# An encoder step with a mixture of experts on one core: low parts on one engine, gate and up weights in 4 KB pieces, token transposes strided, one reordering

## The chip, the cores and the metric

The kernel runs on one core of one Trainium2 chip. The metric is device time in microseconds (us). The kernel before took 510.84 us (median of three runs, 509.73 to 511.15). Engines are called PE (TensorE, matrix products; PEld is its loading of the stationary operand), DVE (VectorE), ACT (ScalarE), POOL (GpSimd) and SP (SyncE, which here only issues transfers).

## What is computed

One layer of a hybrid encoder on 544 tokens (512 of a prompt, 32 of a running stream), width 1024: norm, one input projection split between a gated position-mixing group and a stick-breaking attention group, output projection, residual, then a mixture of experts. All arrays are float32. The change touches only the last part:

```python
def hier_moe(x, w_router_group, b_router_group, w_router_expert, b_router_expert,
             w_gate, w_up, w_down):                      # x (544, 1024) after a norm
    ...                                                  # top group of 4, top 2 of its 4 experts
    combine = ...                                        # (544, 16): gate of each chosen expert
    hg = jnp.einsum('nd,edf->nef', xf, w_gate)           # w_gate, w_up (16, 1024, 256)
    hu = jnp.einsum('nd,edf->nef', xf, w_up)
    a = jax.nn.silu(hg) * hu * combine[:, :, None]
    y = jnp.einsum('nef,efd->nd', a, w_down)             # w_down (16, 256, 1024)
```

## The kernel before

Up to about 295 us the kernel does projection, mixing, attention, output projection and router. Then it runs the 16 experts (E = 16) one after another, each on up to 96 (CAP) gathered token rows. A second round for experts with more than 96 tokens exists in the code and is not run with this input.

**Split products.** A float32 product is made of three passes of a faster format (`three_passes`, L1474 to L1477): high part of x by high part of w, high by low, low by high. The high part of a weight is an ACT copy that rounds (`whi`, L943), the low part is raw minus high (`wlo`, L1350 on DVE).

**Units.** Weights are cut into 48 units of 128 x 2048 values (1 MB), three for each expert: two with half of the 1024 input rows each, gate and up columns side by side, and one with w_down. Expert i uses units 3i - 1 and 3i for gate and up (expert 0: units 0 and 1) and unit 3i + 4 for down (the last: unit 47). SP loads them in the order of their numbers into 12 raw buffers (`moe_loads`, L402): each unit is two DMAs of 512 KB, and from unit 12 on it is issued only when the unit two before it has landed (`few_in_flight`, L446) and its raw buffer is free. High and low parts have three buffers each, so the high part of unit u waits until PE has used unit u - 3 (`hi`, L937).

**Tokens.** POOL gathers the rows of expert i + 2 from DRAM (`gather`, L621), PE transposes them in 8 pieces of 96 x 128 (`turn_tokens`, L1750), ACT and DVE make their high and low parts (`tokens_hi`, L945; `tokens_lo`, L1353).

**Order.** Each engine has its own list of work, in program order; semaphores join them. One step i of PE: gate and up, first half of expert i (12 matmuls of 512 columns); transposes of the activations of expert i - 1; second half (12); transposes of the tokens of expert i + 1; down of expert i - 1 (12). DVE in step i: low part of unit 3i + 1, but only its first 1024 columns; `act_lo`; low part of unit 3i + 2; `tokens_lo` of expert i + 1; `times_up`; low part of unit 3i + 3; `out_rows` (half of the down result from PSUM). ACT has the same order with the high parts. POOL in step i: gather of expert i + 2, low part of the second 1024 columns of unit 3i + 1 (`lo`, L639; semaphore `m_lo_pool`, for which PE's `down` waits), store of the rows of expert i - 2.

Step 0 differs: ACT and DVE make the parts of unit 3 ahead of the parts of expert 1's tokens.

After the last expert POOL gathers the two result rows of each token, and DVE adds them to the residual.

Of the kernel before, what the change touches and what calls it, by code (L numbers as in the profile page):

```python
# [25 lines left out]
F32 = mybir.dt.float32  # L26
# [3 lines left out]
P = 128  # L30
# [4 lines left out]
def trunk_step(nc, x_prompt, x_sample, cache_k, cache_v, norm1_g, w_in, gm_v_norm_g, gm_w_s, gm_b_s,  # L35
# [13 lines left out]
    UK = 4  # L49
# [22 lines left out]
    with ExitStack() as ctx:  # L72
# [157 lines left out]
        m_hi, m_lo, m_lo_pool, m_used = sem("m_hi"), sem("m_lo"), sem("m_lo_pool"), sem("m_used")  # L230
# [105 lines left out]
        def _(sp_):  # L336
# [65 lines left out]
            def moe_loads(r):  # L402
# [26 lines left out]
                def first(m):  # L429

                    i = (m + 1) // 3
                    if not isinstance(r, int):
                        if m % 3 == 1:
                            sp_.wait_ge(m_lo_pool, (E + 1) * r - 4 + m // 3)
                            sp_.sem_inc(sp_tick, 1)
                        elif m == NRAW - 1:
                            sp_.wait_ge(m_lo_pool, (E + 1) * r)
                            sp_.sem_inc(sp_tick, 1)
# [14 lines left out]
                def step(i, b):  # L453
# [5 lines left out]
                    sp_.wait_ge(m_lo_pool, (E + 1) * r + i - 3)  # L459
                    sp_.sem_inc(sp_tick, 1)  # L460
# [12 lines left out]
                sp_.wait_ge(m_lo_pool, (E + 1) * r + E - 4)  # L473
                sp_.sem_inc(sp_tick, 1)
# [17 lines left out]
        def _(pool):  # L492
# [109 lines left out]
            def lo_unit(m, c):  # L602

                return pool.tensor_tensor(wlo[SPLIT_OF[m]][:, c], eraw[m][:, c], whi[SPLIT_OF[m]][:, c].bitcast(F32), ALU.subtract)

# [4 lines left out]
            def moe_gathers(r):  # L610
                s0, u0 = E * r, 3 * E * r
                first = isinstance(r, int)

                if not first:
                    for m in range(3):
                        pool.wait_ge(m_hi, u0 + m + 1)
                        pool.sem_inc(pool_tick, 1)
                        lo_unit(m, slice(0, UNIT)).then_inc(m_lo, 1)
                    pool.sem_inc(m_lo_pool, 1)
                    pool.wait_ge(idx_ok, r + 3)  # L620
                    pool.sem_inc(pool_tick, 1)  # L621
# [17 lines left out]
                def lo(i, j, a):  # L639

                    m = 3 * i + 1 if not (isinstance(i, int) and i == E) else 3 * E - 1
                    slot = unit_at(i, 2, j, a)[0] if not (isinstance(i, int) and i == E) else (3 * E - 1) % NRAW
                    split = SPLIT_OF[1] if not (isinstance(i, int) and i == E) else SPLIT_OF[2]
                    pool.wait_ge(m_hi, u0 + m + 1)
                    pool.sem_inc(pool_tick, 1)
                    pool.tensor_tensor(wlo[split][:, D:2 * D], eraw[slot][:, D:2 * D], whi[split][:, D:2 * D].bitcast(F32),  # L646
                                       ALU.subtract).then_inc(m_lo_pool, 1)

# [6 lines left out]
                def step(i, j, a, p):  # L655
# [3 lines left out]
                    if not (isinstance(i, int) and i == 0):  # L659
                        lo(i, j, a)  # L660
# [7 lines left out]
                if first:  # L668
                    pool.sem_inc(m_lo_pool, 1)
# [7 lines left out]
                lo(E, 0, 0)  # L677
# [30 lines left out]
        def _(act):  # L708
# [225 lines left out]
            def moe(r):  # L934
# [41 lines left out]
                def step(i, j, a):  # L976
# [41 lines left out]
        def _(dve):  # L1018
# [850 lines left out]
```

## Time and profile before

| | |
|---|---|
| median of 3 runs | 510.84 us (509.73 to 511.15) |
| the profiled execution | 510.6 us, its span 509.0 us |
| PE busy | 439.7 us, 86% |
| DVE busy | 285.5 us, 56% |
| ACT busy | 256.4 us, 50% |
| POOL busy | 181.6 us, 36% |
| granted TensorE clock, mean | 0.943 of full |
| HBM read, written | 81.27 MB, 13.04 MB |

The span is the time on the hardware profiler's record; the profiled execution took 1.6 us more than its span. Busy shares are over the whole span, of which the experts are the part from about 306 to 476 us, so a stage has to be read from its own rows. In rows of the timeline the first two numbers are start and length in us; what stands in brackets is the idle time of the engine just before, and who ended it. Matmuls overlap: one of 512 columns is shown as 0.39 us while the next starts 0.23 us after it.

### The profile page before, as it was taken

The page shows a single profiled execution, that of the slowest core. Times are in us where ns is not written, and L with a number is a line of the kernel's source. Part 1 is how long each engine was busy: PE and PEld are TensorE (multiplying, and loading weights), DVE is VectorE, ACT ScalarE, POOL GpSimd, SP SyncE. Part 2 cuts the span into 40 slices and gives each one's busy share as a digit, 9 for nine tenths or more (in the row PEclk, how much of TensorE's full clock was granted, in tenths as well). Part 3 has the DMA queues.
Part 4 walks back from the last instruction along what each step waited for, and adds up shares of the span by engine and source line. Part 5 has one row for each costly group of instructions (what it writes and reads, how often), then busy time and mean ns, then how long its engine had stood idle before and what let it go on. Part 6 is the DMA issues. An engine that isn't in the chain of part 4 may idle for free. (4 is left out here: it accounts for less than half of the span.)

```text
span 509.0 us, 7334 instructions
## 1 busy us (share of the span) xinstructions
PE 439.7 (86%) x2599; PEld 328.6 (65%) x2599; DVE 285.5 (56%) x434; ACT 256.4 (50%) x366; POOL 181.6 (36%) x186
## 2 busy tenths in 40 slices
PE   5999999999698999999999953899999999998200
PEld 4877877787586666667788742577666666665100
DVE  3535542355633645552230256489899999977136
ACT  4664333563434636462135642578777777765100
POOL 0383000514300000000123833456776776745070
PEclk9999999999989999999999965899999999999755
DMA  8872222223214000001595289899999999995276
GB/s 256 219 239 95 89 84 82 84 84 102 78 73 169 3 1 1 1 0 42 194 361 177 107 300 319 249 293 338 328 297 312 332 330 337 344 342 193 68 263 263
DMA packets 64486, 94.80 MB, mean 186 GB/s; under 512 B 11632, under 2 KB 44400, under 8 KB 64448
## 3 DMA queue, kind: packets, MB, share of 16 engines
q1 hardware_dynamic: 55376, 69.87, 43.0%
q0 software_dynamic: 5088, 17.89, 11.2%
q10 hardware_dynamic: 3984, 6.56, 3.6%
q8 instruction: 20, 0.33, 0.3%
q14 instruction: 18, 0.15, 0.1%
HBM read 81.27 MB, written 13.04 MB: 185 GB/s over the span
## 5 line engine op out<-in xcount | busy, mean ns | idle before, releaser
L1350 DVE TENSOR_TENSOR wlo<-raw,whi 128x2048 fp32r<-128x2048 f32 (+1 forms) x47 | 103.7, 2207 | 20.1 <-ACT whi L943 20.0
L1475 PE MATMUL bank<-whi,xT_hi 128*128 128x512 f32 x224 | 93.1, 416 | 3.1 <-DVE wlo L1041 2.2
L943 ACT ACTIVATE whi<-raw 128x2048 fp32r<-128x2048 f32 x45 | 86.2, 1915 | 10.5 <-PE bank L1477 5.5
L1477 PE MATMUL bank<-whi,xT_lo 128*128 128x512 f32 x224 | 88.8, 397 | 0.0
L1476 PE MATMUL bank<-wlo,xT_hi 128*128 128x512 f32 x224 | 88.6, 395 | 0.0
L646 POOL TENSOR_TENSOR wlo<-raw,whi 128x1024 fp32r<-128x1024 f32 x16 | 59.1, 3692 | 38.2 <-ACT whi L943 38.2
L1475 PE MATMUL bank<-whi,xsT_hi 128*96 128x512 f32 x128 | 52.5, 411 | 2.7 <-DVE xsT_lo L1356 2.7
L1476 PE MATMUL bank<-wlo,xsT_hi 128*96 128x512 f32 x128 | 51.4, 401 | 0.0
L1475 PEld LDWEIGHTS bank<-whi,xT_hi 128*128 128x128 f32 x224 | 42.7, 191 | 13.4 <-issue 4.1
L1477 PE MATMUL bank<-whi,xsT_lo 128*96 128x512 f32 x128 | 51.1, 399 | 0.0
L1477 PEld LDWEIGHTS bank<-whi,xT_lo 128*128 128x128 f32 x224 | 42.7, 191 | 9.7
L1476 PEld LDWEIGHTS bank<-wlo,xT_hi 128*128 128x128 f32 x224 | 42.9, 192 | 8.0
L1041 DVE SCALAR_TENSOR_TENSOR wlo<-raw,g_col,whi 128x512 fp32r<-128x512 f32 x40 | 27.9, 752 | 28.6 <-ACT whi L722 21.8
L570 POOL DMA_DIRECT2D g2b<-in_norm_g_dram x1 | 0.6, 642 | 98.8 <-PE bank L1626 98.8
L722 ACT ACTIVATE whi<-raw,g_col 128x512 fp32r<-128x512 f32 x36 | 23.0, 710 | 22.8 <-PE bank L1500 19.2
L509 POOL TENSOR_SCALAR ssq<-ssq 128x1 f32<-128x1 f32 (+3 forms) x20 | 4.0, 202 | 84.3 <-DVE ssq L1153 64.6
L1475 PE MATMUL bank<-whi,aT_hi 128*96 128x512 f32 x64 | 26.1, 408 | 4.9 <-issue 3.6
L1475 PEld LDWEIGHTS bank<-whi,xsT_hi 128*96 128x96 f32 x128 | 21.1, 164 | 12.5 <-DVE xsT_lo L1356 3.9
L1477 PEld LDWEIGHTS bank<-whi,xsT_lo 128*96 128x96 f32 x128 | 21.1, 165 | 9.4
L1476 PEld LDWEIGHTS bank<-wlo,xsT_hi 128*96 128x96 f32 x128 | 21.1, 165 | 7.2
L1477 PE MATMUL bank<-whi,aT_lo 128*96 128x512 f32 x64 | 25.2, 394 | 0.0
L1476 PE MATMUL bank<-wlo,aT_hi 128*96 128x512 f32 x64 | 25.1, 393 | 0.0
(212 smaller groups left out, 766.8 us busy)
## 6 DMA issues: line engine op xcount, KB each, us to landing
raw<-in_w_gate_dram SPq DMA_DIRECT2D x32, 512.0 KB, 6.6
raw<-in_w_up_dram SPq DMA_DIRECT2D x32, 512.0 KB, 8.2
raw<-in_w_down_dram SPq DMA_DIRECT2D x32, 512.0 KB, 6.7
raw<-in_w_in_dram SPq DMA_DIRECT2D x9, 1024.0 KB, 5.1
expert_rows<-yout POOLq DMA_DIRECT2D x16, 384.0 KB, 5.7
raw<-in_w_out_dram SPq DMA_DIRECT2D x4, 1024.0 KB, 5.9
x_sb<-in_x_prompt_dram SPq DMA_DIRECT2D x8, 256.0 KB, 5.9
normed_tokens<-xn ACTq DMA_DIRECT2D x4, 512.0 KB, 3.9
```

Of the source, the lines that this page charges most:

```text
L509: link(pool.tensor_scalar(s, s, 1.0 / width, EPS, ALU.mult, ALU.add))
L570: pool.dma_start(g2b[:, :], norm2_g.broadcast_to([P, D])).then_inc(ld_g2, 16)
L646: pool.tensor_tensor(wlo[split][:, D:2 * D], eraw[slot][:, D:2 * D], whi[split][:, D:2 * D].bitcast(F32), ALU.subtract).then_inc(m_lo_pool, 1)
L722: ins = act.activation(whi[n % 2][:, c], raw[n % 3][:, c], ACT.Copy, scale=g1_col[:, kk:kk + 1])
L943: act.activation(whi[SPLIT_OF[m3]][:, :], eraw[slot][:, :], ACT.Copy).then_inc(m_hi, 1)
L1041: return dve.scalar_tensor_tensor(out=dst, in0=src, scalar=g1_col[:, kk:kk + 1], in1=hi.bitcast(F32), op0=ALU.mult, op1=ALU.subtract)
L1350: dve.tensor_tensor(wlo[SPLIT_OF[m3]][:, 0:n], eraw[slot][:, 0:n], whi[SPLIT_OF[m3]][:, 0:n].bitcast(F32), ALU.subtract).then_inc(m_lo, 1)
L1475: pe.matmul(acc, x_hi, w_hi, start=start, stop=False)
L1476: pe.matmul(acc, x_hi, w_lo, start=False, stop=False)
L1477: return pe.matmul(acc, x_lo, w_hi, start=False, stop=stop)
```

## The change

Four things change in the expert part.

1. The low part of every unit is made wholly by DVE (128 x 2048); POOL makes none in the loop, and `m_lo_pool` with its waits on PE and SP is gone. (POOL still makes the low part of unit 0, before the loop.)
2. A gate or up transfer takes, for partition p, the rows 8p + 4 half to 8p + 4 half + 3 of the weight, which lie together in DRAM: one piece of 4 KB where there were four of 1 KB. Row 8p + c of the weight is then in partition p, so the tokens must be transposed to match: piece c of the transposes reads every eighth column of the gathered rows (a step of 32 bytes) where it read 128 neighbouring ones.
3. In the raw buffer the 4 x 256 gate values stand ahead of the 4 x 256 up values, so a gate and up matmul reads its 512 columns as two runs of 256.
4. In step 0 ACT and DVE make the parts of expert 1's tokens ahead of the parts of unit 3.

```diff
@@ -389,10 +389,9 @@
                 load_unit(n)
 
             def load_gate_up(e, half, slot):
-                dst = eraw[slot][:, :].rearrange("p (k n) -> p k n", k=UK)
                 for j, w in enumerate((w_gate, w_up)):
-                    src = w[0, e, half * UK * P:(half + 1) * UK * P, :].rearrange("(k p) f -> p k f", p=P)
-                    sp_.dma_start(dst[:, :, j * FF:(j + 1) * FF], src).then_inc(m_ld[slot], 16)
+                    src = w[0, e, :, :].rearrange("(p c) f -> p (c f)", c=KC)[:, half * UK * FF:(half + 1) * UK * FF]
+                    sp_.dma_start(eraw[slot][:, j * UK * FF:(j + 1) * UK * FF], src).then_inc(m_ld[slot], 16)
 
...
@@ -456,8 +448,6 @@
                     few_in_flight(i, b, 0)
                     gate_up_unit(i, 1, m, 3 * b)
                     few_in_flight(i, b, 1)
-                    sp_.wait_ge(m_lo_pool, (E + 1) * r + i - 3)
-                    sp_.sem_inc(sp_tick, 1)
                     down_unit(i - 1, m + 1, 3 * b + 1)
                     few_in_flight(i, b, 2)
                     gate_up_unit(i + 1, 0, m + 2, 3 * b + 2)
...
                 def store(i, p):
                     s = s0 + i
                     pool.wait_ge(y_act, s + 1)
@@ -656,8 +624,6 @@
 
                     if not (isinstance(i, int) and i >= E - 2):
                         gather(i + 2, p)
-                    if not (isinstance(i, int) and i == 0):
-                        lo(i, j, a)
                     if not (isinstance(i, int) and i < 2):
                         store(i - 2, p)
...
@@ -983,10 +946,10 @@
                         act_hi(i - 1, 1 - p)
                     if not first:
                         hi(2, unit_at(i, 3, j, a), u0 + 3 * i + 2)
+                    if not last:
+                        tokens_hi(i + 1, 1 - p)
                     if first:
                         hi(0, unit_at(i, 4, j, a), u0 + 3)
-                    if not last:
-                        tokens_hi(i + 1, 1 - p)
                     silu(i, p)
                     if not first and not last:
                         hi(0, unit_at(i, 4, j, a), u0 + 3 * i + 3)
...
             def moe(r):
                 s0, u0 = E * r, 3 * E * r
 
-                def lo(m3, slot, unit, n=UNIT):
+                def lo(m3, slot, unit):
 
                     dve.wait_ge(m_hi, unit + 1)
-                    dve.tensor_tensor(wlo[SPLIT_OF[m3]][:, 0:n], eraw[slot][:, 0:n], whi[SPLIT_OF[m3]][:, 0:n].bitcast(F32),
+                    dve.tensor_tensor(wlo[SPLIT_OF[m3]][:, :], eraw[slot][:, :], whi[SPLIT_OF[m3]][:, :].bitcast(F32),
                                       ALU.subtract).then_inc(m_lo, 1)
...
@@ -1379,15 +1342,14 @@
                     last = isinstance(i, int) and i == E - 1
                     p = i % 2 if isinstance(i, int) else (3 + a) % 2
                     if not first:
-                        lo(1, unit_at(i, 2, j, a)[0], u0 + 3 * i + 1, UNIT // 2)
+                        lo(1, unit_at(i, 2, j, a)[0], u0 + 3 * i + 1)
                         act_lo(i - 1, 1 - p)
                     if not first:
-                        lo(2, unit_at(i, 3, j, a)[0], u0 + 3 * i + 2, UNIT // 2 if last else UNIT)
-                    if first:
-                        dve.wait_ge(m_lo, u0 + 3)
-                        lo(0, unit_at(i, 4, j, a)[0], u0 + 3)
+                        lo(2, unit_at(i, 3, j, a)[0], u0 + 3 * i + 2)
                     if not last:
                         tokens_lo(i + 1, 1 - p)
+                    if first:
+                        lo(0, unit_at(i, 4, j, a)[0], u0 + 3)
                     times_up(i, p)
                     if not first and not last:
                         lo(0, unit_at(i, 4, j, a)[0], u0 + 3 * i + 3)
...
                     dve.tensor_copy(idx_all[:, :], bank[5][0:CAP, 0:E]).then_inc(idx_ok, 1)
-                    tokens_lo(0, 0)
+                    lo(0, 0, u0)
                 else:
                     dve.wait_ge(m_lo, 1)
-                    lo(1, 1, 1)
-                    tokens_lo(0, 0)
-                    lo(2, 2, 2)
+                lo(1, 1, u0 + 1)
+                tokens_lo(0, 0)
+                lo(2, 2, u0 + 2)
...
@@ -1759,7 +1721,7 @@
                             pe.wait_ge(xsT_lo_ok, 2 * s - 1 + b)
                         for k in range(4):
                             mm = pe.transpose(bank[5 + b][:, k * CAP:(k + 1) * CAP],
-                                              xs[p][:, (4 * b + k) * P:(4 * b + k + 1) * P], ident[0:CAP, 0:CAP])
+                                              xs[p][:, :].rearrange("s (q c) -> s c q", c=KC)[:, 4 * b + k, :], ident[0:CAP, 0:CAP])
                         mm.then_inc(xs_tr, 1)
...
                 def gate_up(i, p, half, m3, unit):
@@ -1771,11 +1733,11 @@
                         else:
                             pe.wait_ge(a_ok, s - 1)
                     pe.wait_ge(m_lo, unit + 1)
+                    w_hi, w_lo = (w[SPLIT_OF[m3]][:, :].rearrange("p (j k f) -> p k j f", j=2, k=UK) for w in (whi, wlo))
                     for k in range(UK):
-                        c = slice(k * CB, (k + 1) * CB)
                         kk = UK * half + k
                         mm = three_passes(bank[p][0:CAP, :], xsT_hi[p][:, kk, :], xsT_lo[p][:, kk, :],
-                                          whi[SPLIT_OF[m3]][:, c], wlo[SPLIT_OF[m3]][:, c], kk == 0, kk == KC - 1)
+                                          w_hi[:, k, :, :], w_lo[:, k, :, :], kk == 0, kk == KC - 1)
                     mm.then_inc(m_used, 1)
...
@@ -1791,7 +1753,6 @@
                     s = s0 + i
                     pe.wait_ge(aT_lo_ok, s + 1)
                     pe.wait_ge(m_lo, unit + 1)
-                    pe.wait_ge(m_lo_pool, (E + 1) * r + i + 2)
```

DVE from the first low part of the loop to `act_lo` of expert 0, before (`wlo` is a low part of weights with its buffer number, `xsT_lo1` that of expert 1's tokens, `sg` is `times_up`):

```order
L1350 TENSOR_TENSOR wlo1<-raw5,whi1 128x2048
L1350 TENSOR_TENSOR wlo0<-raw6,whi0 128x2048
L1356 TENSOR_TENSOR xsT_lo1<-bank5,xsT_hi1 128x384
L1356 TENSOR_TENSOR xsT_lo1<-bank6,xsT_hi1 128x384
L1362 TENSOR_TENSOR sg0<-sg0,bank0 96x256
L1350 TENSOR_TENSOR wlo2<-raw7,whi2 128x1024
L1366 TENSOR_TENSOR aT_lo0<-bank7,aT_hi0 128x192
```

and of the changed kernel:

```order
L1313 TENSOR_TENSOR wlo1<-raw5,whi1 128x2048
L1319 TENSOR_TENSOR xsT_lo1<-bank5,xsT_hi1 128x384
L1319 TENSOR_TENSOR xsT_lo1<-bank6,xsT_hi1 128x384
L1313 TENSOR_TENSOR wlo0<-raw6,whi0 128x2048
L1325 TENSOR_TENSOR sg0<-sg0,bank0 96x256
L1313 TENSOR_TENSOR wlo2<-raw7,whi2 128x2048
L1329 TENSOR_TENSOR aT_lo0<-bank7,aT_hi0 128x192
```

The two instructions on expert 1's tokens have moved ahead of unit 3 (`raw6`), and unit 4 (`raw7`) is done over its whole 2048 columns.

POOL in one step of the loop, before (`idx_cur` are the row numbers for the gather into `xs`, `expert_rows` the stored results):

```order
L630 COPY idx_cur0<-idx_all 96x1
L631 REGISTER_ALU
L636 DMA xs0<-normed_tokens,idx_cur0 96x1024
L644 ISA
L646 TENSOR_TENSOR wlo2<-raw4,whi2 128x1024
L653 ISA
L653 DMA expert_rows<-yout0 96x1024
```

and of the changed kernel:

```order
L608 COPY idx_cur0<-idx_all 96x1
L609 REGISTER_ALU
L614 DMA xs0<-normed_tokens,idx_cur0 96x1024
L619 REGISTER_ALU
L621 ISA
L621 DMA expert_rows<-yout0 96x1024
```

Between the gather and the store POOL has no arithmetic left.

## Rows read from the trace of the kernel before

**Rows 1.** Busy time of engines in a stretch, x instructions, TensorE clock, DMA share, GB/s.

```profile
core 0: us, PE busy (x) PEld busy (x) DVE busy (x) ACT busy (x) POOL busy (x), PEclk, DMA share, GB/s
400.00:410.00 10.00, 9.78 (x50) 6.91 (x49) 9.36 (x9) 7.88 (x9) 7.30 (x5) 1.00 1.07 338
```

**Rows 2.** Timeline of PE: token transposes and the first matmul of down, twice.

```profile
331.69 0.82 PE L1761 MATMUL bank<-ident,xs 96*128 96x96 f32 x8
332.30 0.45 PE L1475 MATMUL bank<-whi,aT_hi 128*96 128x512 f32 x1
...
340.88 0.83 PE L1761 MATMUL bank<-ident,xs 96*128 96x96 f32 x8
341.72 0.44 PE L1475 MATMUL bank<-whi,aT_hi 128*96 128x512 f32 x1
```

**Rows 3.** Timeline of PE, later: the first matmul of down of three experts.

```profile
447.20 0.45 PE L1475 MATMUL bank<-whi,aT_hi 128*96 128x512 f32 x1 [0.23 <-issue]
...
467.73 0.44 PE L1475 MATMUL bank<-whi,aT_hi 128*96 128x512 f32 x1 [1.07 <-issue]
472.02 0.47 PE L1475 MATMUL bank<-whi,aT_hi 128*96 128x512 f32 x1 [1.13 <-DVE aT_lo L1366]
```

**Rows 4.** Timeline of DVE and POOL in one step.

```profile
392.82 2.28 DVE L1350 TENSOR_TENSOR wlo<-raw,whi 128x2048 fp32r<-128x2048 f32 x1
...
395.27 3.82 POOL L646 TENSOR_TENSOR wlo<-raw,whi 128x1024 fp32r<-128x1024 f32 x1 [1.85 <-ACT whi L943]
...
395.62 1.21 DVE L1350 TENSOR_TENSOR wlo<-raw,whi 128x1024 fp32r<-128x1024 f32 x1
...
397.81 3.43 DVE L1350 TENSOR_TENSOR wlo<-raw,whi 128x2048 fp32r<-128x2048 f32 x1 [0.71 <-ACT whi L943]
```

**Rows 5.** Timeline of PE, ACT and DVE around the first matmul of expert 1.

```profile
324.01 0.39 PE L1477 MATMUL bank<-whi,xsT_lo 128*96 128x512 f32 x1
325.91 0.47 PE L1475 MATMUL bank<-whi,xsT_hi 128*96 128x512 f32 x1 [1.50 <-DVE xsT_lo L1356]
...
321.07 1.92 ACT L943 ACTIVATE whi<-raw 128x2048 fp32r<-128x2048 f32 x1 [5.48 <-PE bank L1477]
...
325.30 1.01 DVE L1356 TENSOR_TENSOR xsT_lo<-bank,xsT_hi 128x384 fp32r<-128x384 f32 x2
```

**Rows 6.** The same view as rows 1, of stretches by what is loaded.

```profile
252.00:262.00 10.00, 10.00 (x77) 8.01 (x76) 4.65 (x8) 3.12 (x4) 0.84 (x2) 1.00 1.10 350
...
311.00:449.00 138.00, 131.09 (x634) 92.71 (x635) 117.39 (x107) 99.37 (x109) 89.83 (x53) 0.96 1.02 316
262.00:264.00 2.00, 2.00 (x13) 1.69 (x13) 0.79 (x4) 0.00 (x0) 1.92 (x2) 1.00 1.07 396
448.00:450.00 2.00, 2.00 (x10) 1.41 (x9) 2.00 (x3) 1.39 (x1) 0.00 (x0) 1.00 1.03 412
```

**Rows 7.** Waits of SP's queue: waited for, us in total, times, longest.

```profile
SPq L451 <- DMA raw<-in_w_up_dram: 60.5, 20, 4.8
```

**Rows 8.** Timeline of SP's queue: first issue of unit 12, last issues.

```profile
307.77 0.39 SPq L395 DMA_DIRECT2D raw<-in_w_gate_dram  x1
...
451.31 2.95 SPq L399 DMA_DIRECT2D raw<-in_w_down_dram  x4
```

**Rows 9.** Timeline of ACT: high parts of units 44 and 47.

```profile
455.83 1.91 ACT L943 ACTIVATE whi<-raw 128x2048 fp32r<-128x2048 f32 x1 [2.33 <-DMA raw<-in_w_up_dram]
...
465.49 1.92 ACT L943 ACTIVATE whi<-raw 128x2048 fp32r<-128x2048 f32 x1 [1.34 <-DMA raw<-in_w_down_dram]
```

**Rows 10.** Timeline of PE and its loads: token transposes at half and at full clock.

```profile
313.55 1.51 PE L1761 MATMUL bank<-ident,xs 96*128 96x96 f32 x8 [8.12 <-DMA xs<-normed_tokens,idx_cur]
...
331.46 0.87 PEld L1761 LDWEIGHTS bank<-ident,xs 96*128 96x128 f32 x8
```

**Rows 11.** The token gathers: time from issue to landing in us.

```profile
DMA to landing us min/median/max: 4.5/7.6/9.3
```

**Rows 12.** The chain that ended last begins here.

```profile
476.31 0.52 DMA expert_rows<-yout
```

More of the change, by code:

```diff
@@ L229, in trunk_step @@
         m_ld = [sem(f"m_ld{i}") for i in range(NRAW)]
-        m_hi, m_lo, m_lo_pool, m_used = sem("m_hi"), sem("m_lo"), sem("m_lo_pool"), sem("m_used")
+        m_hi, m_lo, m_used = sem("m_hi"), sem("m_lo"), sem("m_used")
         xs_ld = [sem(f"xs_ld{i}") for i in range(2)]
@@ L431, in first @@
                     i = (m + 1) // 3
-                    if not isinstance(r, int):
-                        if m % 3 == 1:
-                            sp_.wait_ge(m_lo_pool, (E + 1) * r - 4 + m // 3)
-                            sp_.sem_inc(sp_tick, 1)
-                        elif m == NRAW - 1:
-                            sp_.wait_ge(m_lo_pool, (E + 1) * r)
-                            sp_.sem_inc(sp_tick, 1)
                     if m < 2:
@@ L458, in step @@
                     few_in_flight(i, b, 1)
-                    sp_.wait_ge(m_lo_pool, (E + 1) * r + i - 3)
-                    sp_.sem_inc(sp_tick, 1)
                     down_unit(i - 1, m + 1, 3 * b + 1)
@@ L472, in moe_loads @@
                 gate_up_unit(E - 1, 1, 3 * E - 3, NRAW - 3)
-                sp_.wait_ge(m_lo_pool, (E + 1) * r + E - 4)
-                sp_.sem_inc(sp_tick, 1)
                 down_unit(E - 2, 3 * E - 2, NRAW - 2)
@@ L600, in _ @@
                         ins.then_inc(m_lo, 1)
-            def lo_unit(m, c):
-                return pool.tensor_tensor(wlo[SPLIT_OF[m]][:, c], eraw[m][:, c], whi[SPLIT_OF[m]][:, c].bitcast(F32), ALU.subtract)
             pool.wait_ge(sel_ok, 2)
@@ L614, in moe_gathers @@
                 if not first:
[L615 to L619, printed above, removed]
                     pool.wait_ge(idx_ok, r + 3)
@@ L637, in gather @@
                                             bass.IndirectOffsetOnAxis(ap=idx_cur[p][:, 0:1], axis=0)).then_inc(xs_ld[p], 16)
[L639 to L647, printed above, removed]
                 def store(i, p):
@@ L667, in moe_gathers @@
                 gather(1, 1)
-                if first:
-                    pool.sem_inc(m_lo_pool, 1)
                 for i in range(3):
@@ L676, in moe_gathers @@
                     step(i, 0, 0, i % 2)
-                lo(E, 0, 0)
                 store(E - 2, 0)
@@ L1381, in step @@
                     if not first:
-                        lo(1, unit_at(i, 2, j, a)[0], u0 + 3 * i + 1, UNIT // 2)
+                        lo(1, unit_at(i, 2, j, a)[0], u0 + 3 * i + 1)
                         act_lo(i - 1, 1 - p)
                     if not first:
-                        lo(2, unit_at(i, 3, j, a)[0], u0 + 3 * i + 2, UNIT // 2 if last else UNIT)
-                    if first:
-                        dve.wait_ge(m_lo, u0 + 3)
-                        lo(0, unit_at(i, 4, j, a)[0], u0 + 3)
+                        lo(2, unit_at(i, 3, j, a)[0], u0 + 3 * i + 2)
                     if not last:
                         tokens_lo(i + 1, 1 - p)
+                    if first:
+                        lo(0, unit_at(i, 4, j, a)[0], u0 + 3)
                     times_up(i, p)
```

## The prediction

> **What bounds the kernel now.** I read the chain of waits first: it begins at 476.31 with the store of the last expert's rows [rows 12], and all behind it (gather of the results, final sum) is untouched. So the question is how much earlier the experts end. Next the windows of the expert loop. The reader is to see three things at once [rows 1]: PE is busy 9.78 of 10 us at full clock, DVE 9.36, and the DMA engines are full (share 1.07, 338 GB/s). Then the timeline of PE, because a full PE can hide small waits. Down of expert 0 starts at 332.30 [rows 2] and down of expert 12 at 447.20 [rows 3]: 114.90 us for 12 steps, 9.575 each. How long is a step without a wait? Where nothing is late, the first matmul of down follows the start of the token transposes by 0.61 (331.69 to 332.30); one step later it follows by 0.84 (340.88 to 341.72) [rows 2]. That step is 9.42 long, of which 0.23 is such a wait, so PE's own work is 9.19. In most later steps down waits more, and the page calls it "issue" [rows 3]. What is it? POOL's half of a low part runs from 395.27 to 399.09 [rows 4], and that step's down begins right behind it. So 0.385 us of each step are a wait for POOL.
>
> The last steps have another cause: from down of expert 12 to down of expert 14 it is 20.53 us [rows 3], and ACT stands waiting for DMAs of weights, 2.33 and 1.34 us [rows 9]. SP in turn waits 60.5 us in all for earlier units to land [rows 7]: loading runs at its own limit and PE has used up the 12 units of lead just before the end.
>
> **The change part by part.** I sum against the profiled execution's own 510.6 us; the median of the runs is 0.2 above it.
>
> *Step 0's order.* PE ends the second half of expert 0 and could start its next matmul at 324.24 (0.23 behind 324.01), but starts at 325.91, because DVE makes expert 1's token parts at 325.30, behind unit 3 [rows 5]. In the changed order ACT makes the token parts before the 1.92 us of unit 3, and DVE too. Gain 1.67. What is late next? Unit 3 itself: ACT about 322.1 to 324.0, DVE 2.28 more to 326.4; PE needs it behind 12 matmuls, at 327.1. It fits by 0.7.
>
> *POOL's low parts go, DVE makes them whole.* PE's down no longer waits for POOL: 12 steps x 0.385 = 4.62. DVE pays 1.07 a step (2.28 for 2048 columns against 1.21 for 1024) and gets back 1.15: the same kind of instruction takes 3.43 where it starts at 397.81 while POOL is still in its own, until 399.09, and 2.28 beside no POOL arithmetic [rows 4]. So DVE's load stays: 9.36 of 10 us is 8.96 a step, less 1.15, plus 1.07, is 8.88 of 9.19. This is what hides the longer instruction, and it is thin cover. Following the in-order lists, I find each low part done before PE wants it: a unit's buffer is free three units ahead, and high part (1.91) plus low part (2.28) take 4.2 of the 6 us until then. If the cover fails, each step is as long as DVE's, which is the third rival. The waits of SP on `m_lo_pool` held nothing the trace shows.
>
> *4 KB pieces.* Gate and up alone move at 350 GB/s in 10 us; where down units (4 KB pieces) dominate, windows show 396 and 412 [rows 6]. I take 400 for the new pieces: 12.5% less time on gate and up, which are 2.1 of the 4.2 MB moved per three units loaded (3.15 MB of weights, the rest gathers and stores at 316 GB/s for the 13.2 us that three units take). So 6.2% less in all. Unit 12 is issued at 307.77 [rows 8] and unit 44's high part starts as it lands, at 455.83 [rows 9]: 148 us, so it lands 9.2 us earlier. Needed: down of expert 13 would start at 332.30 - 1.67 + 13 x 9.19 = 450.1, gate and up of expert 15 at 452.9, minus 2.28 and 1.92 for low and high part: 448.7, 7.1 us earlier than now. It fits by 2 us. Unit 47 needs about as much. Then the last two steps take 2 x 9.19 - 0.61 (no more tokens to transpose) = 17.77 for 20.53: gain 2.76. The 4.29 us from there to the last down [rows 3] are a chain through ACT and DVE that the change leaves as it is.
>
> A page speaks to this price. The Trainium skill, DMA: Bandwidth & Descriptors, "Why small descriptors are slow (HBM only)", gives about 3 extra cycles per piece over 32 bytes a cycle; an estimate from it is 35 cycles for 1 KB and 131 for 4 KB, 6.4% less instead of 12.5%. The rows show more than that. By the page the units would land 4.7 us earlier where 7.1 are needed, and the time would be 505.0.
>
> *First gather.* PE's first transposes wait until 313.55 for it [rows 10]. It competes with weights in other piece sizes than before. The gathers took 4.5 to 9.3 us, this one 6.9, near the middle of 7.6 [rows 11]: I take no change and keep -2.4 and +2.4 as ends.
>
> *Strided transposes.* 16 sets of 8 now load their stationary operand with a step of 32 bytes. No row shows such a read. The 8 loads take 0.87, more than the 0.61 that PE gives a set, and begin 0.23 ahead, under the last matmul [rows 10, 2]: they pace the set. Lower end: nothing, or a little below if pieces of one row lie better, which I count as nothing. Upper end, the nearest row of a slow set: at half clock it takes 1.51 instead of 0.83, 0.69 more [rows 10, 2]. I take 0.05 a set (0.8 in all), near the row of the same instruction with the same shape, and keep 0.69 for the range.
>
> *Two runs of 256 columns in the matmuls.* Same columns, same passes; nothing, at most 0.01 on each of 384, below 4 us.
>
> Sum: 510.6 - 1.67 - 4.62 - 2.76 + 0.8 = 502.4; as a median 502.6.
>
> **The rivals.**
> *The strided loads are dear (slower).* Mechanism: each of 8 loads in a set fetches one value at a time from scattered places, loads pace the set, PE has no slack [rows 1]. Price 0.69 on 15 sets at full clock, twice that on the first: 11.7. Time 510.6 - 9.05 + 11.7 = 513.3; sooner PE's units lose their lateness too, so a little above 512.5 is as likely. It decides from 9.05/17 = 0.53 us a set. For it: loads, not matmuls, pace this set. Against it: it is a small read, 128 values in 0.11 us, half the pace of a moving operand (512 in 0.23).
> *Weights stay the bound.* If the mix of pieces, gathers and stores is limited by something else than piece size (windows beside gathers fall to 316), units 44 to 47 land when they did. Then only what lies between lands and end is left: down of the last expert about 0.8 earlier, 509.8. Half the gain in rate gives 505. Against it: 350 against about 400 with nothing else changed.
>
> *DVE becomes the bound.* 8.88 of 9.19 leaves 0.3. If POOL's row-number copies and its gathers' preparation cost DVE 0.4 a step or the order adds waits, steps stay 9.575: 510.6 - 1.67 - (20.53 - 18.54) + 0.8 = 507.7. For it: DVE waited 0.71 for ACT in each step as it was [rows 4].
>
> **How the numbers follow.** Forecast (499.5 to 504.5) 0.55; weights the bound 0.12 (505 to 510); DVE the bound 0.11 (505 to 508); strided loads dear 0.22, of which 0.14 above 512.4, 0.05 between and 0.03 below. A measurement of this kernel tells 0.3% (1.5 us) from no change: faster is below 509.3, which is 0.55 + 0.09 + 0.11 + 0.03 = 0.78; same 0.03 + 0.05 = 0.08; slower 0.14. The low end is the forecast with the gather's -2.4 and less stride: 499.5. The high end takes in most of the slow rival: 513.0. The forecast's own range is 499.5 to 504.5.
>
> **What would show it.** Right: down starts about 9.2 us apart with no "issue" wait before it; DVE's 2048-column low parts all at 2.28; expert 1's first matmul without a wait for `xsT_lo`; windows of gate and up loads near 400 GB/s and no wait of ACT for weights at the end; 8 transposes in about 0.85. Wrong: transposes of 1.3 us or more with longer loads (first rival), ACT waiting for DMAs behind 440 us (second), PE waiting for `wlo` each step (third). What would break the forecast most easily is the stride.

## The result, and the profile after

| | before | after |
|---|---|---|
| median | 510.99 us (11 runs, 509.32 to 517.8) | 508.21 us (11 runs, 503.35 to 510.25) |
| ratio of the two | | 0.9933 (0.9906 to 0.996) |
| profiled execution, its span | 510.6, 509.0 | 510.25, 508.6 |
| POOL busy | 181.6 us | 112.8 us |
| DVE busy | 285.5 us | 290.0 us |
| DMA packets | 64486 | 39908 |

Medians are of all runs; a ratio and its 95% interval leave out slow runs, those more than 1.5% above the fastest of the same kernel.

The ratio says 0.7% faster, 3.4 us (2.0 to 4.8; 2.8 by the medians), where 8.2 were forecast. The profiled execution happens to be the longest of the eleven; so the traces are read for where time goes, and the medians for how much.

First the part of the loop that went as foreseen. Timeline of PE in the changed kernel, two steps, the token transposes and the first matmul of down (answers to [rows 2]):

```profile
378.52 1.02 PE L1723 MATMUL bank<-ident,xs 96*128 96x96 f32 x8
379.32 0.45 PE L1437 MATMUL bank<-whi,aT_hi 128*96 128x512 f32 x1
...
387.88 1.02 PE L1723 MATMUL bank<-ident,xs 96*128 96x96 f32 x8
388.69 0.45 PE L1437 MATMUL bank<-whi,aT_hi 128*96 128x512 f32 x1
```

A step is 9.36 to 9.37, no down waits, and down follows the start of the transposes by 0.80 where it was 0.61 without a wait: 9.19 plus 0.18 for the stride. The windows of the same trace (answer to [rows 1] and [rows 6]; times, busy us with instruction counts, clock, DMA share, GB/s):

```profile
252.00:262.00 10.00, 10.00 (x74) 7.97 (x73) 4.03 (x8) 2.75 (x3) 1.28 (x1) 1.00 1.00 387
262.00:264.00 2.00, 2.00 (x15) 1.78 (x14) 1.63 (x4) 0.37 (x2) 1.46 (x2) 1.00 1.01 401
...
311.00:449.00 138.00, 132.57 (x638) 96.31 (x638) 119.27 (x107) 99.61 (x108) 30.84 (x40) 0.96 0.98 318
400.00:410.00 10.00, 10.00 (x50) 7.30 (x49) 9.35 (x10) 8.19 (x9) 2.80 (x4) 1.00 1.00 335
```

PE is busy 10.00 of 10, DVE 9.35 as before. Gate and up alone now move at 387 GB/s in the window where they moved at 350. (In 304 to 308 us it is 420 after 396, but that stretch holds a down unit too.) But over the 138 us of the loop it is 318 after 316: where it counts, the larger pieces brought next to nothing. What SP waits for (us in total, times, longest) and its issue of unit 44 show the same ([rows 7, 8]). First two rows of the kernel before that stand beside the one in [rows 7], then the changed kernel:

```profile
SPq L451 <- DMA raw<-in_w_down_dram: 30.0, 11, 6.6
...
SPq L460 <- POOL wlo L646: 5.2, 2, 3.3
```
```profile
SPq L443 <- DMA raw<-in_w_up_dram: 67.2, 21, 4.6
...
SPq L443 <- DMA raw<-in_w_down_dram: 34.3, 10, 8.6
```
```profile
449.42 0.33 SPq L394 DMA_DIRECT2D raw<-in_w_gate_dram  x1
```

SP waited 101.5 us for landings after 90.5. Unit 12 was issued at 308.14, so 32 units took 141.3 us, 4.41 each. Before it was 307.77 to 448.75: 4.41 as well. PE came earlier to the end of its lead and found the weights where they had been. Timeline of ACT (high parts of units 40, 41, 42 and 44) and then of PE from there on (answer to [rows 9] and [rows 3]):

```profile
440.54 1.92 ACT L906 ACTIVATE whi<-raw 128x2048 fp32r<-128x2048 f32 x1 [1.38 <-DMA raw<-in_w_down_dram]
...
445.12 1.91 ACT L906 ACTIVATE whi<-raw 128x2048 fp32r<-128x2048 f32 x1 [2.46 <-DMA raw<-in_w_up_dram]
...
449.29 1.91 ACT L906 ACTIVATE whi<-raw 128x2048 fp32r<-128x2048 f32 x1 [1.23 <-DMA raw<-in_w_up_dram]
...
457.33 1.92 ACT L906 ACTIVATE whi<-raw 128x2048 fp32r<-128x2048 f32 x1 [3.54 <-DMA raw<-in_w_up_dram]
```
```profile
449.97 0.47 PE L1437 MATMUL bank<-whi,xsT_hi 128*96 128x512 f32 x1 [1.68 <-DVE xsT_lo L1319]
...
453.58 0.47 PE L1437 MATMUL bank<-whi,xsT_hi 128*96 128x512 f32 x1 [0.42 <-DVE wlo L1313]
...
462.10 0.57 PE L1437 MATMUL bank<-whi,xsT_hi 128*96 128x512 f32 x1 [1.84 <-DVE xsT_lo L1319]
...
473.69 0.47 PE L1437 MATMUL bank<-whi,aT_hi 128*96 128x512 f32 x1 [1.13 <-DVE aT_lo L1329]
```

Unit 44's high part starts as the unit lands: at 457.33, where it was 455.83 and was to be 9.2 us earlier. The name behind PE's wait, `xsT_lo`, is the last link only: ACT's lists are in order, and its token parts stand behind the high part that waited for the DMA. Behind the 1.84 us wait the granted clock also fell: 0.58 and 0.56 of 2.4 GHz in these windows, so most of them at the lower level, 1.2 GHz: eight matmuls there start 0.43 us apart instead of 0.23. Behind the wait of 1.68 us it had not fallen.

```profile
462.00:464.00 2.00, 1.90 (x5) 1.34 (x6) 2.00 (x4) 1.53 (x3) 0.00 (x0) 0.58 0.97 397
464.00:466.00 2.00, 2.00 (x6) 1.31 (x6) 2.00 (x3) 1.65 (x1) 0.00 (x0) 0.56 0.17 70
```

One difference had not been thought of. The chain that ended last, behind the store of the last rows ([rows 12]; start, us, what): before, then after.

```profile
480.99 0.06 POOLq L695
481.05 3.28 issue
484.33 1.01 POOL raw L688
```
```profile
482.61 0.06 POOLq L658
482.67 1.18 issue
483.85 1.00 POOL raw L651
```

Between POOL's branch and its first gather of results lie 3.28 us before and 1.18 after: 2.1 us won outside the loop.

The two traces, then, from PE's first transposes (313.55 and 315.00) on: order of step 0, -1.5; steps up to the last three, -2.0; the last three, +3.7; the end behind the last matmul, -2.1; and the changed kernel's execution began the experts 1.5 later, 0.8 of it before the first gather was issued. That is the -0.4 between these two executions.

### The profile page after: what moved, and what is told of

The parts are those of the page before. It is cut to its first block and busy times, and to the rows that moved or that the text cites. A ratio compares the mean times of both kernels' runs of the same rounds, so it can differ in the third digit from the quotient of the medians.

```text
span 508.6 us, 7272 instructions
## 1 busy us (share of the span) xinstructions
PE 442.5 (87%) x2599; PEld 333.3 (66%) x2599; DVE 290.0 (57%) x434; ACT 257.0 (51%) x366; POOL 112.8 (22%) x170
## 2 busy tenths in 40 slices
DMA packets 39908, 94.78 MB, mean 186 GB/s; under 512 B 11632, under 2 KB 11632, under 8 KB 39872
## 3 DMA queue, kind: packets, MB, share of 16 engines
q0 software_dynamic: 5088, 17.89, 10.9%
## 5 line engine op out<-in xcount | busy, mean ns | idle before, releaser
L1313 DVE TENSOR_TENSOR wlo<-raw,whi 128x2048 fp32r<-128x2048 f32 x47 | 107.6, 2289 | 14.8 <-ACT whi L906 14.6
L914 ACT ACTIVATE xsT_hi<-bank 128x384 fp32r<-128x384 f32 x32 | 14.7, 489 | 25.9 <-PE bank L1723 25.7
L621 POOL DMA_DIRECT2D expert_rows<-yout x16 | 8.6, 540 | 77.0 <-DVE yout L1337 73.0
L1723 PE MATMUL bank<-ident,xs 96*128 96x96 f32 x128 | 16.8, 277 | 8.8 <-DMA xs<-normed_tokens,idx_cur 8.8
```

Of the source, the lines that this page charges most:

```text
L621: pool.dma_start(y_dram[bass.ds(r * SLOTS + i * CAP, CAP), :], yout[p][:, :]).then_inc(y_st[p], 16)
L914: act.activation(xsT_hi[p][:, 4 * b:4 * b + 4, :].rearrange("p k n -> p (k n)"), bank[5 + b][:, 0:4 * CAP], ACT.Copy).then_inc(xsT_hi_ok, 1)
L1313: dve.tensor_tensor(wlo[SPLIT_OF[m3]][:, :], eraw[slot][:, :], whi[SPLIT_OF[m3]][:, :].bitcast(F32), ALU.subtract).then_inc(m_lo, 1)
L1723: mm = pe.transpose(bank[5 + b][:, k * CAP:(k + 1) * CAP], xs[p][:, :].rearrange("s (q c) -> s c q", c=KC)[:, 4 * b + k, :], ident[0:CAP, ...
```

## Experiments

Each is timed beside the kernel before. "Four in flight" is one number: SyncE waits, before it issues a unit, for the landing of the unit AHEAD places back.

**Less to load.** Does the end still belong to the weights?

```diff
+                n = D if isinstance(e, int) and e < 4 else D // 8
                 for k in range(2):
-                    sp_.dma_start(eraw[slot][:, k * D:(k + 1) * D], w_down[0, e, k * P:(k + 1) * P, :])
+                    sp_.dma_start(eraw[slot][:, k * D:k * D + n], w_down[0, e, k * P:(k + 1) * P, 0:n])
```

> The changed kernel, but of the down weights of experts 4 to 15 only the first 128 of 1024 columns are loaded (10.5 MB of 50 left out; the outputs of these experts are not the reference's). Theory W (the weights' transfers still set the end: 4.41 us a unit in both traces, so the 9.37 us steps run into late weights in the last two experts): without them the tail's waits (1.9 + 7.8 us of ScalarE for down and up loads) go, the clock doesn't fall there, and the time is 502 to 503.5, about 5 under the changed kernel's 508.2. Rival S (the stride and the later first gather ate the gain, the tail's waits are by the way): 507 to 508.

503.12 us, ratio 0.982 (0.9774 to 0.9867): theory W, 5.1 under the changed kernel. Steps are 9.37 to the end, and from the last transposes to the last matmul it is 16.6 us where it was 20.3. Yet the loads hardly went out faster: unit 44 was issued at 447.52 after unit 12 at 313.20, 4.20 us each, with the DMA engines at 275 GB/s and a share of 0.90 (340 to 420 us), and SyncE waited 79.9 us for the landings of gate and up alone. Three units thus took 12.6 us; at the 336 GB/s of the changed kernel their bytes would have taken about 10 (an estimate from these two rates).

**Four in flight.**

```diff
-    AHEAD = 2
+    AHEAD = 4
```

> The changed kernel with four units in flight instead of two behind the weights' queue. Theory W1 (the weights are late because SyncE waits for the unit before the last to land before it issues the next): the unit's period falls from 4.41 to about 3.5 us and the time to 503 to 505. Theory W2 (the rate is what the memory gives beside gathers and stores, whatever is queued): 4.3 to 4.5 us a unit, 507.5 to 509.

504.3 us, 0.9855 (0.9807 to 0.9904). W1, with a unit's period of 3.94 us where 3.5 was expected. Window of 80 us in the middle of the loop, and the issue of unit 44 with it; first the changed kernel's window, then with four in flight:

```profile
340.00:420.00 80.00, 80.00 (x396) 58.54 (x395) 75.62 (x71) 64.08 (x70) 19.18 (x26) 1.00 1.01 336
```
```profile
340.00:420.00 80.00, 80.00 (x396) 58.55 (x395) 76.11 (x70) 64.28 (x69) 18.88 (x27) 1.00 1.02 371
```
```profile
428.20 0.33 SPq L394 DMA_DIRECT2D raw<-in_w_gate_dram  x1
```

Unit 44 goes out 21 us earlier. Part of that is only that it no longer waits for units 41 and 42. Like for like, unit 40 had landed by 428.20, and with two in flight its landing let unit 42 go at 440.59: at least 12 us. Over the whole trace SyncE waits 49.5 us for landings instead of 101.5, and now nearly as long for a raw buffer to come free (the row of DVE `wlo`, 10.4 before), which is as far ahead as the loads can be:

```profile
SPq L418 <- DVE wlo L1313: 41.8, 16, 7.5
SPq L443 <- DMA raw<-in_w_up_dram: 32.6, 14, 3.5
...
SPq L443 <- DMA raw<-in_w_down_dram: 16.9, 7, 3.5
```

The DMA share is the same 1.0 at 336 and at 371 GB/s: that share did not tell that the engines could move more.

**Old pieces and transposes, two in flight.** The line below, with the transposes and the matmuls' columns as before:

```diff
-                    src = w[0, e, :, :].rearrange("(p c) f -> p (c f)", c=KC)[:, half * UK * FF:(half + 1) * UK * FF]
+                    src = w[0, e, half * UK * P:(half + 1) * UK * P, :].rearrange("(k p) f -> p k f", p=P)
```

> The changed kernel with the weights in 1 KB pieces and the token transposes of neighbouring columns, as before; the order and the low parts on VectorE stay. Steps of 9.19 us instead of 9.37. Theory W: the weights land at the old rate, the end stays with them, 507 to 509.5, the same as with 4 KB pieces. Rival P (4 KB pieces do bring the weights sooner, the stride costs what was read): without both, steps 2.6 us shorter in sum but the tail some 3 to 6 us longer, 509 to 512.

510.13 us, 0.9922 (0.9879 to 0.9964), runs from 503.3 to 511.8. By the median this is 1.9 above the changed kernel, by the ratio level with it (0.9933): with two in flight the two sizes of piece can't be told apart, and so neither can the two theories. In the trace steps are 9.19, but the last two take 9.65 and 12.09; unit 44 goes out at 448.19 where it was 449.42, and 340 to 420 us show 328 GB/s where it was 336. So what the shorter steps save is waited for at the end, or what the larger pieces bring pays for their stride; the runs leave both open, at 2 us or so.

**Pieces and strides alone.** The kernel before with these lines of the change, the strided transposes, and the matmuls' columns to match:

```diff
-                    src = w[0, e, half * UK * P:(half + 1) * UK * P, :].rearrange("(k p) f -> p k f", p=P)
+                    src = w[0, e, :, :].rearrange("(p c) f -> p (c f)", c=KC)[:, half * UK * FF:(half + 1) * UK * FF]
```

> The kernel before with only the 4 KB pieces and the strided transposes; GpSimd keeps its low parts and the order its place. The stride's 0.19 us a set lies ahead of the down matmuls that wait 0.385 us for GpSimd, so steps stay 9.6 us. Theory W (pieces bring little in the loop): 510 to 511.5. Rival P (they bring the weights sooner): the tail falls by up to 2.8 us, 508 to 509.

510.6 us, 0.9976 (0.9946 to 1.0006): not told from no change. Its steps are 9.6 us: the stride is hidden under the wait for GpSimd.

**The kernel before with four in flight.**

```diff
-    AHEAD = 2
+    AHEAD = 4
```

> The kernel before with four units in flight. If the changed kernel's parts are worth what their rows say once the weights are on time (order 1.67, GpSimd's low parts 4.62, less 14 sets of strided transposes at 0.19 = 2.6; sum 3.7), this ends 3.7 us above the changed kernel with four in flight (504.3), at about 508: only its tail gets shorter, by 2 to 3 us, its steps stay 9.6 us. Rival: the rule is worth to the kernel before what it is to the changed one, 4 us or more, and ends at 505 to 507.

511.82 us, 1.0011 (0.9993 to 1.0029): a miss for both, nothing is gained. From its trace: the last transposes to the last matmul 18.09 after 19.26, the first gather 7.6 us after 7.0 (one trace each). The kernel before was hardly bound by the rule; its steps are paced by GpSimd.

**Four in flight, 1 KB pieces, neighbouring columns.** The edit of "old pieces" above, and AHEAD = 4.

> Four in flight, the weights in 1 KB pieces and the transposes of neighbouring columns, the rest as changed. Theory L (the piece's size doesn't bound the loop, the rule did): steps of 9.19 us with the weights on time, 501.5 to 502.5, below the changed kernel with four in flight. Rival P (1 KB pieces carry 350 GB/s at most with nothing beside them, 320 to 335 beside gathers and stores, where 4 KB pieces now carry 385): the weights stay late, the unit's period is 4.0 us or more and the time 505 to 508.

502.0 us, 0.9827 (0.9802 to 0.9853). Theory L for the time. Rival P was right on the rate: unit 44 goes out at 436.01, a period of 4.18 us, where 4 KB pieces had 428.20, and 340 to 420 us show 348 GB/s for 371. That was still early enough. SyncE itself is busy longer, too: its issue of 512 KB takes up to 5.66 us here, 0.33 to 0.44 for the last units with 4 KB pieces. Against the 511.82 of the kernel before with four in flight, the change is worth 9.8 us without the pieces and the stride, and 7.5 with them.

**The stride alone.**

```diff
-                                              xs[p][:, :].rearrange("s (q c) -> s c q", c=KC)[:, 4 * b + k, :], ident[0:CAP, 0:CAP])
+                                              xs[p][:, (4 * b + k) * P:(4 * b + k + 1) * P], ident[0:CAP, 0:CAP])
```

> Four in flight and 4 KB pieces, but the token transposes read neighbouring columns (so the tokens' columns don't match the weights' rows, and the experts' outputs are not the reference's). Prices the stride alone: 14 sets at 0.19 us = 2.6, so 501.7 if the stride lies wholly on TensorE's path as the 9.37 and 9.19 us steps say; 504.3 if something else fills the step.

502.18 us, 0.9867 (0.9819 to 0.9915), steps 9.19: the stride costs 2.1 us by the medians, 2.5 by 14 steps of 0.18. The ratios don't show it (0.9855 with the stride): two of the six runs here took 507.0 and 508.8 at a granted clock of 0.935 and 0.933, the others 501.4 to 502.7. The line's weight loads (ns, min/median/max), strided and not:

```profile
L1723 PEld LDWEIGHTS bank<-ident,xs x128: 186/204/231, 315.0 to 457.1; 96*128 96x128 f32 x128
```
```profile
L1723 PEld LDWEIGHTS bank<-ident,xs x128: 138/142/230, 315.7 to 451.7; 96*128 96x128 f32 x128
```

**Old order, four in flight.** In ACT's list, and likewise in DVE's:

```diff
-                    if not last:
-                        tokens_hi(i + 1, 1 - p)
                     if first:
                         hi(0, unit_at(i, 4, j, a), u0 + 3)
+                    if not last:
+                        tokens_hi(i + 1, 1 - p)
```

> Four in flight, the changed kernel, but unit 3's high and low parts are made ahead of the second expert's tokens again, as before. If the order is worth the wait that it removed (1.5 to 1.7 us, with nothing late behind it), 504.3 + 1.6 = 505.9. If the tokens of the second expert are late anyway (the first gather lands later with the weights in larger pieces), 504.3.

506.22 us, 0.991 (0.9886 to 0.9933): 1.9 over the changed kernel with four in flight (2.8 by the ratios). The order's gain is real.

**The order alone, two in flight.** The kernel before with the lines of the last diff the other way round:

```diff
-                    if first:
-                        hi(0, unit_at(i, 4, j, a), u0 + 3)
                     if not last:
                         tokens_hi(i + 1, 1 - p)
+                    if first:
+                        hi(0, unit_at(i, 4, j, a), u0 + 3)
```

> The kernel before with only the order of step 0 changed. The order is worth 1.5 to 1.9 us of TensorE's time. Theory W (two units in flight set the end): the weights of the last experts come when they came, and of the gain 0.3 to 1 us arrives: 510.5 to 511.2. Rival: the weights of the kernel before are just on time (its last step is only about 1.2 us longer than with four in flight), and the gain arrives whole: 509.6.

510.59 us, 0.9989 (0.9964 to 1.0013): of 1.9 us, 0.6 arrives (-0.7 to 1.8), which can be told neither from nothing nor quite from the whole. Its trace speaks against theory W: one step is 1.7 shorter and the last is 19.15 after 19.26, so from the first transposes to the last matmul the gain arrives whole, 1.8 us. This execution began the experts 1.0 later, 0.6 of it in the first gather (7.6 us after 7.0).

**GpSimd's low parts alone, four in flight.** The kernel before, and in VectorE's list (GpSimd's `lo` and all waits on `m_lo_pool` go):

```diff
-                        lo(1, unit_at(i, 2, j, a)[0], u0 + 3 * i + 1, UNIT // 2)
+                        lo(1, unit_at(i, 2, j, a)[0], u0 + 3 * i + 1)
```

> The kernel before with four units in flight and only GpSimd's low parts moved to VectorE (1 KB pieces, old order). If the parts add up (511.8 with four in flight and nothing else, 502.0 with the order, 1.9, as well): 503.9, so GpSimd's parts are worth 7.9 us: 0.4 in each of 13 steps, 1.5 in the last, 2.1 behind the last matmul (GpSimd's wait ahead of its last gathers, 3.3 us in the kernels that have its low parts and 1.2 in those without). If only the steps' part is real: 506.5 to 507.

503.66 us, 0.9845 (0.9818 to 0.9873). The sum held: 8.2 us under the 511.82 that differ from it in nothing else. The part forecast at 4.62 is the largest of all. One of its seven runs took 510.73. That is the one traced: its last two steps are 10.83 and 13.36, so with 1 KB pieces four in flight are not always enough.

**Units 10 and 11 wait for the first gather.** With 1 KB pieces, then with 4 KB pieces, four in flight:

```diff
+                    if m == 10 and isinstance(r, int):
+                        sp_.wait_ge(xs_ld[0], 16)
```

> The fastest so far (1 KB pieces, neighbouring columns, four in flight, the order and VectorE's low parts), and units 10 and 11 are not asked for until the first gather of tokens has landed. That gather takes 7.0 to 8.6 us from its issue to the first transposes with six units of weights queued beside it. Theory G (it shares the DMA engines with them): 5 us or less, 498.5 to 500. Rival (its time is its own 96 rows and GpSimd's making of descriptors): 502 as before, or above if the weights asked for later come late.

> The same wait in the changed kernel with four in flight (4 KB pieces, strided transposes). Theory G: its first gather took 8.6 us, so 504.3 falls by 3 to 4 us, to 500 to 501.5. Rival: 504.3 or more.

503.65 us (0.9853, 0.9825 to 0.9881) and 499.94 us (0.9768, 0.9741 to 0.9795). With 4 KB pieces theory G holds, with 1 KB pieces its time does not. But in both traces the first gather is quicker, 4.4 and 4.5 us from issue to the first transposes after 8.2 and 8.6: it did share its time with the weights. PE's first transposes in the kernel with 4 KB pieces, where the changed kernel had waited 8.75 and the same with four in flight 9.70 (answer to [rows 10]):

```profile
311.97 1.51 PE L1725 MATMUL bank<-ident,xs 96*128 96x96 f32 x8 [5.62 <-DMA xs<-normed_tokens,idx_cur]
```

With 1 KB pieces the start is as early (311.81) but the last three steps take 39.6 us instead of 35.1: those weights are late. Here the 4 KB pieces decide.

**The columns turned when the tokens are stored.** The stride goes to GpSimd's product with the norm's gain, the transposes read neighbouring columns:

```diff
-                pool.tensor_tensor(xn2[t][0:rows[t], c], x_sb[0:rows[t], t, c], g2b[0:rows[t], c], ALU.mult).then_inc(hg_ok, 1)
+                turned = xn2[t][0:rows[t], :].rearrange("p (c q) -> p q c", c=KC)[:, half * P // 2:(half + 1) * P // 2, :]
+                x_, g_ = (v.rearrange("p (q c) -> p q c", c=KC) for v in (x_sb[0:rows[t], t, c], g2b[0:rows[t], c]))
+                pool.tensor_tensor(turned, x_, g_, ALU.mult).then_inc(hg_ok, 1)
```

> 4 KB pieces, four in flight, units 10 and 11 held, and the stride taken off TensorE: GpSimd writes the normed tokens with their columns already in the order of the weights' rows, the transposes read neighbouring columns. Steps of 9.19 us: 499.9 less 14 x 0.18 = 497.4. Rival: the weights, just on time at 9.37 us a step, are late at 9.19 (as 1 KB pieces were, 503.7), or GpSimd's strided writes delay the first gather: 499 to 502.

498.27 us, 0.9741 (0.9714 to 0.9769): the fastest of all, 2.6% under the kernel before, with steps of 9.19 and no weight late. It is 1.7 under the last one where 2.5 were expected. The strided writes cost GpSimd nothing (start, us):

```profile
287.28 1.30 POOL L567 TENSOR_TENSOR xn<-x_sb,g2b 128x512 f32<-128x512 f32 x1
```
```profile
287.57 1.31 POOL L565 TENSOR_TENSOR xn<-x_sb,g2b 128x512 f32<-128x512 f32 x1
```

The first is strided, the second of the kernel above it is not.

**Three in flight.** The changed kernel:

```diff
-    AHEAD = 2
+    AHEAD = 3
```

> The changed kernel with three units in flight. Theory W1 (the rule holds the loads back): the unit's period falls from 4.41 us to between 3.7 and 4.1, the tail's 6.6 us of late weights to 0 to 2: 504 to 506. If only four bring it: 507.5 to 508.5.

504.51 us, 0.988 (0.9839 to 0.9921): three do what four do. Unit 44 goes out at 435.96, and 340 to 420 us show 357 GB/s, between 336 and 371.

**GpSimd's low parts alone, two in flight.** The edit of "four in flight" above without its AHEAD.

> The kernel before with only GpSimd's low parts moved to VectorE, two in flight. Worth 7.9 us with four in flight. Theory W: the weights land when they did, so of the 5 us ahead of them nothing arrives, and of the 2.1 us behind the last matmul all and of the last step's 1.5 some: 508 to 509.5. Rival: the parts' sum, 504.

511.16 us by the median of twelve, 0.1 under the kernel before; 0.9952 (0.992 to 0.9985) by the ratio, 2.5 us (0.8 to 4.1). So of 8.2 us two in flight leave something between nothing and half. The runs scatter from 504.3 to 515.3, and the trace is of the longest: its last steps take 13.92, 10.12 and 13.77 us, waiting for weights.

**The held units with two in flight.** The changed kernel with

```diff
+                    if m == 10 and isinstance(r, int):
+                        sp_.wait_ge(xs_ld[0], 16)
```

> The changed kernel, two in flight, units 10 and 11 held back until the first gather has landed. TensorE starts 3 to 4 us earlier, the weights come at the same period and no earlier. Theory W: all of it is waited for at the end, 507.5 to 510. Rival: 504.5.

513.33 us, 1.0018 (0.9992 to 1.0045): 5 us above the changed kernel (4.3 by the ratios), worse than theory W. PE starts at 311.10, but five steps from 402 us on are 10.9 to 12.4 long; unit 44 goes out at 453.73. A wait that wins 4.4 us with four in flight loses 4 to 5 with two.

## Why the prediction was wrong

The failed step is the one on the 4 KB pieces: "148 us, so it lands 9.2 us earlier. Needed: ... 7.1 us earlier than now. It fits by 2 us." Unit 44 was issued at 449.42 after 448.75 and landed at 457.33 after 455.83, no earlier. What set the pace of the loads was not the size of their pieces but SyncE's rule of two units in flight: a unit took 4.41 us before and after, 4.12 with three in flight and 3.94 with four. The second rival, "weights stay the bound", was what happened; it had a chance of 0.12. Its full form said 509.8; less the 2.1 us at POOL's branch, which neither it nor the forecast had seen, that is 507.7, near the 508.2 measured. Point by point:

- *Step 0's order*, forecast 1.67: 1.9 with the weights on time; by itself with two in flight 1.8 in the one trace, 0.6 (-0.7 to 1.8) in the runs.
- *POOL's low parts*, forecast 4.62: 8.2 with the weights on time. The steps gave what was said, 0.39 each over 12 to 13. Not seen were 2.1 us at POOL's branch and about 1.5 in the last step, where POOL's half part stood ahead of PE too (18.09 with it, 16.62 without). DVE's load stayed as worked out, and no step waited for it: the third rival did not occur. "The waits of SP on `m_lo_pool` held nothing the trace shows" was a misreading: the row of 5.2 us above is that wait, two of them between 320 and 360 us. Without it unit 44 went out no earlier, so it cost nothing there.
- *4 KB pieces*, forecast 2.76 for on-time weights, measured as late weights: the last three steps are 3.7 longer. The failure was to carry a rate read from windows into a loop in which SyncE issues a unit when the one two places back has landed. The waits of 60.5 us in [rows 7] (90.5 with those for down) were taken for "loading runs at its own limit". The row says only that the queue's issuer waited; whether engines or the rule set the pace it cannot say, and three or four in flight settled it. With two in flight unit 44 goes out at 448.19 with 1 KB pieces and at 449.42 with 4 KB; with four at 436.01 and 428.20, so there the larger pieces bring 7.8 us of lead, much of the 9.2 that were forecast, to units that are no longer late. The size of the rate was too high as well: in 252 to 262 us the kernels with 4 KB pieces show 381 to 392 GB/s after 350 to 352, 8 to 11% less time, not 12.5. The 396 of [rows 6] was a window of 2 us, in which kernels with 1 KB pieces show anything from 358 to 396. The estimate of 6.4%, worked out from the Trainium skill's 3 cycles a packet (DMA: Bandwidth & Descriptors, "Why small descriptors are slow (HBM only)"), is below what these traces show. With two in flight neither would have given a right time.
- *First gather*, forecast 0: 7.0 us from issue to transposes before, 7.6 after, one trace each; inside the ends given. Holding back units 10 and 11 was worth 4.4 us with four in flight and 4 KB pieces.
- *Strided transposes*, forecast 0.8: 2.1 to 2.5. The cost per set is 0.18, not 0.05 and far from the 0.53 from which the first rival decides. The rule of the Trainium skill (Advanced Engine Details and Errata, "SBUF Cachelines"), a penalty where each access goes to another line, agrees in sign. The page gives no factor; "about twice" was the prediction's own, and each strided load took 204 ns after 142, 1.4 times.
- *Two runs of 256 columns*: with the weights on time, 4 KB pieces with plain transposes and 1 KB pieces end alike (502.18 and 502.0), so nothing that shows.

The sum of what the parts are worth with weights on time is 8.2 + 1.9 - 2.1 = 8.0 against 511.82, and the measured difference is 7.5. With three in flight the changed kernel takes 504.51, at the edge of the forecast's own range. That would have been luck: GpSimd's part taken too small would have made up for the stride taken too cheap and for pieces worth nothing. With two, about 4 of it went into ACT's waits for weights and the slow clock behind them.

Open: why the DMA engines, at a share of 1.0 in both, move 336 GB/s with two in flight and 371 with four. In 340 to 420 us the weights' queue took 74.5% of the engines for 20.04 MB with two and 77.4% for 22.93 MB with four, 9% less engine time for a MB; no run took the gathers or the stores away to see whether they make the difference. Open too is what POOL does in the 2.1 us. The gap behind its branch is 3.3 to 3.4 us in the four traces with GpSimd's low parts and 1.2 in the fourteen without, and with four in flight the pair of 511.82 and 503.66 us differs in those low parts alone, so they make it. Each long gap holds two packets of 8 KB on a queue of kind "instruction", each short one at most one. That POOL loads code for its branch fits, but was not tried by itself.

## What to carry to other kernels

Where a queue's issuer waits for landings, treat the number in flight as a bound of its own, and try it before pricing any gain that reaches the end of a prefetch: the same edit was worth 8.2 us with four in flight and, by the median or by the ratio, 0.1 or 2.5 with two. A gain on the engine that consumes a prefetch is paid only as far as the lead lasts; so compare when the last units are issued and land, not rates in a window. And a permutation cost nothing here where an instruction writes each value once and has time (GpSimd's product), and 0.18 us a step in front of TensorE, which was busy 80.00 of 80 us.

## What the runs showed of the hardware

- A stationary load of 96 x 128 fp32 with a step of 32 bytes takes 204 ns after 142; eight of them lengthen a set of transposes from 0.82 to 1.02 us.
- GpSimd writes 512 values a row at a step of 512 bytes in 1.30 us, neighbouring ones in 1.31.
- The first gather reached its transposes 4.4 to 4.6 us after its issue where units 10 and 11 were held back, and 7.6 to 8.6 in the same kernels where they were not.
- With four units in flight, 4 KB pieces moved 371 GB/s beside gathers and stores and 1 KB pieces 348; with two, 336 and 328.
- One issue of 512 KB kept SyncE busy up to 5.66 us with 1 KB pieces and four units in flight, at most 0.44 for the last units with 4 KB pieces.
- A DMA share of 1.0 went with 336 as with 371 GB/s.
- Behind POOL's branch it took 3.3 to 3.4 us to the first gather with the low parts in its program (four traces), 1.2 without (fourteen).
